# Turning the inputs of three phases with VectorE and DMAs instead of TensorE

## What is computed

```python
h   = norm(x) * gain                      # with modulation: norm(x) * gain * (1 + scale) + shift
hdn = (silu(h @ w_gate) * (h @ w_up)) @ w_down
x   = x + 0.5 * norm(hdn) * gain_post
# second block
mod     = silu(c)     @ ada_w + ada_b     # 9 vectors of 1024
mod_ctx = silu(c_ctx) @ ada_w + ada_b
x   = macaron_ffn(x, mod[0:3], ...)
ctx = macaron_ffn(ctx, mod_ctx[0:3], ...)
h_f, h_b = context_states(ctx, mod_ctx[3:6], ...)
x   = mix_sublayer(x, mod[3:6], h_f, h_b, ...)
x   = macaron_ffn(x, mod[6:9], ...)
```

## Time and profile before

| | us |
|---|---|
| median of three runs | 1662.7 |
| lowest and highest | 1661.25, 1665.88 |
| profiled execution | 1663.65 |
| its span, first to last instruction | 1661.9 |
| granted TensorE clock in it | 1.000 |

### The profile page before, as it was taken

One profiled execution on the slowest core, in us unless ns is written; L12 is line 12 of the kernel. 1 busy time (PEld: TensorE's weight loads), 2 busy tenths in 40 slices (PEclk: granted clock), 3 DMA queues, 4 the chain that ended last, 5 costly groups with the idle time before them and its releaser, 6 DMA issues.

```text
span 1661.9 us, 22791 instructions
## 1 busy us (share of the span) xinstructions
PE 1651.5 (99%) x8748; PEld 1419.4 (85%) x8748; DVE 1217.4 (73%) x1632; ACT 925.1 (56%) x1396; POOL 156.2 (9%) x210
## 2 busy tenths in 40 slices
PE   9999999999999999999999999999999999999998
PEld 7888888888888888888899888888888889988887
DVE  6888776788888767776688776655765668986564
ACT  6655577554545455455566455554555558665553
POOL 1100100000311000120010010100002012310000
PEclk9999999999999999999999999999999999999999
DMA  8977553787859876687646457654667646357561
GB/s 293 337 261 256 170 197 103 240 293 257 285 169 328 272 249 222 246 303 257 201 161 198 164 177 265 199 183 147 219 217 245 195 137 203 111 177 245 181 198 65
DMA packets 99356, 358.47 MB, mean 216 GB/s; under 512 B 11184, under 2 KB 11696, under 8 KB 99248
## 3 DMA queue, kind: packets, MB, share of 16 engines
q1 hardware_dynamic: 92736, 334.73, 60.1%
q0 software_dynamic: 6368, 22.21, 4.1%
q10 hardware_dynamic: 144, 0.07, 0.0%
HBM read 355.85 MB, written 1.12 MB: 215 GB/s over the span
## 4 chain that ended last, share of the span: by engine, by line
PE 94%; DMA 2%; DVE 2%; ACT 1%; issue 0%; SPq 0%; DVEq 0%; POOLq 0%; POOL 0%; ACTq 0%
PE dn L573 28%; PE gu L503 19%; PE tp L544 10%; PE gu L544 10%; PE tp L551 5%; PE gu L551 5%; PE dn L518 5%; DMA raw<-in_weights 2%; PE tp L531 1%; PE gu L531 1%; PE tp L466 1%; PE dn L544 1%; DVE w_lo L1829 1%; PE gu L518 1%; DVE w_lo L1836 1%; PE tp L536 1%
## 5 line engine op out<-in xcount | busy, mean ns | idle before, releaser
L1836 DVE TENSOR_TENSOR w_lo<-raw,w_hi 128x1024 fp32r<-128x1024 f32 x518 | 633.6, 1233 | 302.4 <-ACT w_hi L1195 298.4
L1195 ACT ACTIVATE w_hi<-raw 128x1024 fp32r<-128x1024 f32 x520 | 547.7, 1056 | 436.6 <-PE gu L551 146.1
L503 PE MATMUL gu<-w_hi,hT 128*128 128x512 f32 x1056 | 328.9, 393 | 1.6 <-DVE w_lo L1829 1.1
L573 PE MATMUL dn<-w_hi,actT_hi 128*128 128x512 f32 x608 | 238.6, 392 | 0.0
L573 PE MATMUL dn<-w_lo,actT_hi 128*128 128x512 f32 x608 | 236.8, 390 | 0.0
L573 PE MATMUL dn<-w_hi,actT_lo 128*128 128x512 f32 x608 | 236.8, 390 | 0.0
L503 PEld LDWEIGHTS gu<-w_hi,hT 128*128 128x128 f32 x1056 | 195.5, 188 | 43.1 <-DVE hT L1844 1.7
L503 PE MATMUL gu<-w_lo,hT 128*128 128x512 f32 x528 | 205.8, 390 | 0.0
L544 PE MATMUL tp<-hT,w_hi 128*128 128x512 f32 x736 | 183.3, 391 | 1.1 <-DVE actT_lo L1844 1.0
L544 PE MATMUL gu<-hT,w_hi 128*128 128x512 f32 x736 | 174.8, 390 | 0.0
L544 PEld LDWEIGHTS gu<-hT,w_hi 128*128 128x128 f32 x736 | 137.8, 188 | 28.6
(11 more groups left out here) (366 smaller groups left out, 1986.2 us busy)
## 6 DMA issues: line engine op xcount, KB each, us to landing
raw<-in_weights SPq DMA_DIRECT2D x561, 512.0 KB, 4.3
arena<-in_ada_w SPq DMA_DIRECT2D x72, 512.0 KB, 4.4
post_row<-in_post_rows POOLq DMA_DIRECT2D x10, 512.0 KB, 5.7
pre_row<-in_pre_rows POOLq DMA_DIRECT2D x10, 512.0 KB, 7.0
mod_row<-mod POOLq DMA_DIRECT2D x9, 512.0 KB, 8.6
shift_row<-mod POOLq DMA_DIRECT2D x5, 512.0 KB, 9.3
x<-in_x_in SPq DMA_DIRECT2D x4, 256.0 KB, 5.6
arena<-in_c_rows POOLq DMA_DIRECT2D x2, 512.0 KB, 8.9
```

Source lines behind the costliest of these rows:

```text
L503: m = pe.matmul(bank, h[:, k, t * P:(t + 1) * P], w[:, r, kk * 512:(kk + 1) * 512], start=k == 0 and q == 0, stop=k == KT - 1 and q == 2)
L573: m = pe.matmul(dn[:, t, c], a[:, k, :], w[:, r, c], start=start and q == 0, stop=stop and q == 2)
L1195: act.activation(o, i, ACT.Copy, **kw).then_inc(done, 1)
L1836: dve.tensor_tensor(w_lo[:, r, :], raw[:, n % RAW, :], w_hi[:, r, :].bitcast(F32), ALU.subtract).then_inc(lo_ready, 1)
```

## The change

Three phases are called `APART`: ctx_ffn, ffn_2 and ctx_mix. For them, in the phase before:

- VectorE scales, normalises and transposes the rows in place in 32x32 blocks (`turned_in_blocks`), one or two operations a step in steps 7, 8 and 9, placed behind the reductions (`ahead`).
- SyncE stores the two tiles (512 KB each) to HBM, one after the load at slot LAST - 9 and one after that at LAST - 3, and after that at LAST - 1 waits for both stores and issues four loads of 256 KB that put the blocks in place in xT, in the arena. A load reads runs of 1 KB.
- Partition c * 32 + i of xT holds feature c * 256 + k * 32 + i for tile k, so the host reorders the rows of the gate, up and mixer input weights of these phases to match (`by_blocks`).
- TensorE's `transposed` and the wait between its two blocks go. In the tail it does both tokens' down products and activation transpositions in one loop.
- ScalarE's upper copies and VectorE's subtractions read xT in SBUF instead of PSUM, and ScalarE waits for all four loads. VectorE's split of the second half of the activations comes before the input split of t = 1, no longer behind it.
- ScalarE's squares of the next input move from step 8 to step 4.
- Steps 7 and 8 of ffn_1 do one reduction instead of two, later ones slide, and the first modulation group is turned after step 4 instead of 6.

```diff
+APART = [s for s in EARLY if s - 1 in FFNS]
+APART_STEP = STEPS - 4
-        ADA_IN[_s, _j] = list(range(_done, min(_done + 2, ADA_N)))
+        _n = 1 if _s == FFNS[1] and _j in (APART_STEP, APART_STEP + 1) else 2
+        ADA_IN[_s, _j] = list(range(_done, min(_done + _n, ADA_N)))
-ADA_TURN = {(FFNS[1], 6): 0, (FFNS[2], 8): 1, (FFNS[3], 9): 2}
+ADA_TURN = {(FFNS[1], 4): 0, (FFNS[2], 8): 1, (FFNS[3], 9): 2}
...
+        xT = part(4480, TT, BLOCKS, KT * BLOCK)
...
+        def in_half(s, t, half):
+
+            if s in APART:
+                return xT[:, t, :, :].rearrange("p a (k j) -> p k a j", k=KT)[:, 4 * half:4 * half + 4, :, :]
+            return in_bank(s, t, half).rearrange("p (k a j) -> p k a j", k=4, a=BLOCKS)
...
+            def turned_store(s, t):
+                sp.wait_ge(blocks_turned, TT * APART.index(s) + t + 1)
+                sp.dma_start(turned[bass.ts(t, P), :], xn[:, t, :]).then_inc(turned_stored, 16)
+
+            def turned_load(s):
+                sp.wait_ge(turned_stored, 16 * TT * (APART.index(s) + 1))
+                rows = turned.rearrange("(t a i) (c m) -> c i t a m", t=TT, a=BLOCKS, c=BLOCKS)
+                for c in range(BLOCKS):
+                    sp.dma_start(xT[c * BLOCK:(c + 1) * BLOCK, :, :, :], rows[c]).then_inc(turned_landed, 16)
...
+                    if s + 1 in APART:
+                        if n in (LAST[s] - 9, LAST[s] - 3):
+                            turned_store(s + 1, (n - LAST[s] + 9) // 6)
+                        if n == LAST[s] - 1:
+                            turned_load(s + 1)
...
-                    transposed(s + 1, 0)
-                    for kk in range(2):
-                        down_slot(end + 4 + kk, tokens_of(actT_hi, actT_lo, [0]), kk, used=False)
-                    half_transposed(STEPS - 1, 0)
-                    hT_there(s + 1, 0)
-                    transposed(s + 1, 1)
-                    for kk in range(2):
-                        down_slot(end + 4 + kk, tokens_of(actT_hi, actT_lo, [1]), kk)
-                    half_transposed(STEPS - 1, 1)
+                    for t in range(TT):
+                        for kk in range(2):
+                            down_slot(end + 4 + kk, tokens_of(actT_hi, actT_lo, [t]), kk, used=t == 1)
+                        half_transposed(STEPS - 1, t)
...
             def in_half_upper(s, t, half):
+                if s in APART:
+                    act.wait_ge(turned_landed, 16 * BLOCKS * (APART.index(s) + 1))
...
-                    if j == STEPS - 3 and s + 1 in EARLY:
+                    if j == 4 and s + 1 in APART:
                         for t in range(TT):
                             in_squares(s + 1, t)
...
+            def turned_in_blocks(s, t):
+                dve.wait_ge(xn_ready, TT * (s - 1) + t + 1)
+                dve.transpose(xn[:, t, :], xn[:, t, :]).then_inc(blocks_turned, 1)
...
+                def ahead(j, q):
+                    if s + 1 not in APART:
+                        return
+                    if j == APART_STEP:
+                        if q == 0:
+                            scaled_apart(0)
+                        else:
+                            normalised(s + 1, 0)
+                    if j == APART_STEP + 1:
+                        if q == 0:
+                            turned_in_blocks(s + 1, 0)
+                        else:
+                            scaled_apart(1)
+                    if j == APART_STEP + 2:
+                        if q == 0:
+                            normalised(s + 1, 1)
+                        else:
+                            turned_in_blocks(s + 1, 1)
...
                         ada(j, 0)
+                        ahead(j, 0)
                         after_slots(n, 1)
                         gates_summed(j)
                         after_slots(n + 1, 2)
                         ups_summed(j)
                         ada(j, 1)
+                        ahead(j, 1)
...
                     in_lower(s + 1, 0)
                     half_lower(STEPS - 1, 0)
                     after_slots(end + 3, 1)
+                    half_lower(STEPS - 1, 1)
                     in_lower(s + 1, 1)
                     after_slots(end + 4, 1)
-                    half_lower(STEPS - 1, 1)
```

More of the change, by code:

```diff
@@ L79 @@
 EARLY = [s for s in range(1, len(SUB)) if SOURCE[s] != s - 1]
+APART = [s for s in EARLY if s - 1 in FFNS]
+TURNED_N = {s: 2 * TT * len([q for q in range(s) if q not in APART]) for s in range(len(SUB))}
+BLOCK = 32
+BLOCKS = P // BLOCK
+APART_STEP = STEPS - 4
 NORMS = [("pre", 0, t) for t in range(TT)]
@@ L136, with build @@
 MIX0 = {"ab": 0, "sc": MIX_AB, "ssd": MIX_AB + MIX_SC}
-def build(nc, weights, ada_w, x_in, ctx_in, pre_rows, post_rows, small, mod, out):
+def build(nc, weights, ada_w, x_in, ctx_in, pre_rows, post_rows, small, mod, turned, out):
     with ExitStack() as stack:
@@ L1258, in in_half_upper @@
             def in_half_upper(s, t, half):
-                act.wait_ge(hT_psum, 2 * (TT * s + t) + half + 1 if s else FIRST_HT[t, half])
-                copy(hT_hi[:, 4 * half:4 * half + 4, t * P:(t + 1) * P],
-                     in_bank(s, t, half).rearrange("p (k c) -> p k c", k=4), hT_hi_ready)
+                if s in APART:
+                    act.wait_ge(turned_landed, 16 * BLOCKS * (APART.index(s) + 1))
+                else:
+                    act.wait_ge(hT_psum, TURNED_N[s] + 2 * t + half + 1 if s else FIRST_HT[t, half])
+                copy(in_half_to(hT_hi, t, half), in_half(s, t, half), hT_hi_ready)
             def in_upper(s, t):
@@ L1404, in ffn @@
                     act_upper(STEPS - 2)
-                if s + 1 in EARLY:
+                if s + 1 in APART:
                     after_slots(end, 3)
@@ L2042, in ada, with scaled_apart @@
                         ada_sums(i)
+                def scaled_apart(t):
+                    if s + 1 in MOD:
+                        in_scaled(s + 1, t)
+                def ahead(j, q):
[14 more added lines that the diff above has]
+                            normalised(s + 1, 1)
+                        else:
+                            turned_in_blocks(s + 1, 1)
                 def first_opening():
@@ L2676, in narrow, with by_blocks, swiglu_slots @@
     return slot
-def swiglu_slots(w_gate, w_up, w_down, turned=True):
+def by_blocks(w):
+    return w.reshape(BLOCKS, KT, BLOCK, -1).transpose(1, 0, 2, 3).reshape(D, -1)
+def swiglu_slots(w_gate, w_up, w_down, turned=True, apart=False):
+    if apart:
+        w_gate, w_up = by_blocks(w_gate), by_blocks(w_up)
     slots = []
@@ L2700 @@
            ffn2_w_gate_2, ffn2_w_up_2, ffn2_w_down_2):
-    first = swiglu_slots(ffn1_w_gate_2[0], ffn1_w_up_2[0], ffn1_w_down_2[0])
+    first = (ffn1_w_gate_2[0], ffn1_w_up_2[0], ffn1_w_down_2[0])
     w_in, dt_at = w_in_2[0], 4 * 256 + 512 + SSD_W + 512
@@ L2709 @@
         "ffn_1": swiglu_slots(ffn2_w_gate[0], ffn2_w_up[0], ffn2_w_down[0]),
-        "ctx_ffn": first,
-        "ffn_2": swiglu_slots(ffn1_w_gate[1], ffn1_w_up[1], ffn1_w_down[1]),
+        "ctx_ffn": swiglu_slots(*first, apart=True),
+        "ffn_2": swiglu_slots(ffn1_w_gate[1], ffn1_w_up[1], ffn1_w_down[1], apart=True),
         "sc": [mixed_columns(c_in, [k * D + i * P for i in range(KT) for k in (1, 2, 0)]), c_w_out[0]],
-        "ctx_mix": [narrow(w_in[:, dt_at:]), columns(w_in[:, 1024 + 512:dt_at])],
+        "ctx_mix": [narrow(by_blocks(w_in[:, dt_at:])), columns(by_blocks(w_in[:, 1024 + 512:dt_at]))],
         "ffn_3": swiglu_slots(ffn2_w_gate[1], ffn2_w_up[1], ffn2_w_down[1]),
-        "ffn_4": first,
+        "ffn_4": swiglu_slots(*first),
         "ssd": [wide(w_in[:, :512]), wide(w_in[:, 512:1024]), narrow(w_in[:, dt_at:]), mixed_columns(w_in, [1024 + i * P for unit in XBC_UNITS[1] for i in unit]),
@@ L2778 @@
     mod = nc.dram_tensor("mod", [ADA_N, 2, P], F32, kind="Internal").ap()
+    turned = nc.dram_tensor("turned", [TOK, D], F32, kind="Internal").ap()
     out = nc.dram_tensor("out", [TOK, D], F32, kind="ExternalOutput").ap()
     build(nc, aps["weights"], aps["ada_w"], aps["x_in"], aps["ctx_in"], aps["pre_rows"], aps["post_rows"],
-          {name: aps[name] for name in small_arrays}, mod, out)
+          {name: aps[name] for name in small_arrays}, mod, turned, out)
     nc.compile()
```

6 lines of the change are left out of this document (4 added, 2 removed).

## The result

The changed kernel takes 1667.4 us (median of 7 runs, 1664.7 to 1669.6), the kernel before 1662.95 beside it on the same chip (7 runs): ratio 1.003, 95% interval [1.002, 1.004]. Forecast were 1659.6 us and a range of 1657.0 to 1666.5. The profiled execution took 1667.38 us with a span of 1665.6; before it was 1663.65 and 1661.9, so the two profiles differ by 3.7 us.

A forecast was written before the change was run, and what follows sets the result against it. TensorE, busy 1651.5 of 1661.9 us, was taken as the bound. From the profiled 1663.65 us, +0.35 - 1.75 - 1.75 = -3.15 gives 1660.5, and the median lies 0.95 below that execution: 1659.6 us, range 1657.0 to 1666.5.

The forecast's parts named there:

- What bounds the kernel, the ceiling: TensorE bounds the kernel; removing two transposition blocks in each of three tails saves at most 5.2 us, 1.75 a tail.
- VectorE's turn: Steps 7 to 9: a 32x32 transposition pass on VectorE takes 1.2 us, at most 2.4, and costs TensorE nothing.
- The moves: Squares to step 4, modulation group after step 4, scaling earlier, reductions shifted: no cost; any modulation shortfall paid once.
- the third rival: Tails: copies from the turned tile slower than from PSUM; doubled, they add 1.2 us a tail, 1663 us; chance 0.08.
- Where TensorE arrives early: Tails into next openings: VectorE's list makes ffn_1 +0.35 us; ctx_ffn and ffn_2 keep -1.75 each.
- The wait of "some 2 us": In ctx_ffn's opening, the first token-turning pair waits some 2 us for VectorE's gate product; in ffn_2's it doesn't.
- The round trip: Tails: second store issued at 459 to 461, loads landed at 467 to 475, taken as 470.5 in ffn_1, in time.
- T: Start of a tail's first block of transpositions, 469.12 in ffn_1; the reference for landing times.
- The first rival: Late round trip in the tails: each us beyond T + 1.9 costs one at all three; worst 1671 us; chance 0.27.
- point of decision: Late loads cost time only from a landing at T + 1.9 on; earlier landings are free.
- some 12 us from store to need: Tails: time available between the store and the copies' need of the loads, given as evidence against a late round trip.

The follow-up runs named there:

- e1: The changed kernel with its loads reading x_in rows, not waiting for the stores, five slots earlier; three phases get wrong inputs: 1659.72 us, ratio 0.9985.
- e3: The changed kernel with the round trip cut by token tile, tile 0 loaded six places earlier behind its own store: 1659.84 us, ratio 0.9982.
- e10: e3 with one VectorE reduction kept in each of ffn_1's steps 9 and 10: 1658.06 us, ratio 0.9973.
- e6: The kernel before with only the moved work of the change, TensorE still transposing: 1662.08 us, ratio 0.9994.
- e8: The changed kernel with the two weight loads behind the second store held until the round trip's loads are issued: 1673.02 us, one run.
- e5: The changed kernel with four more loads (768 KB, to an unused place) ahead of the real ones in each tail: 1681.45 us, ratio 1.0115.
- e11: The changed kernel with the second store issued one place earlier, ahead of the weight load just before it: 1667.35 us, ratio 1.0031.
- e2_list: The changed kernel with the two reductions of ffn_1's step 10 done in its steps 7 and 8: 1666.89 us, ratio 1.0026.

## Why the prediction was wrong

**What bounds the kernel, the ceiling.** Right. TensorE without the blocks is 1.8 us earlier per tail, in one case 2.3, where neither the loads nor VectorE's list are late (e1, e3), and e10 has 5.5 us in the stretches and 4.1 in the medians, of a ceiling of 5.2.

**VectorE's turn.** Right: 1.24 us each, against 1.2 taken, and no product waited for it. The Trainium skill (VectorE: DVE Perf Modes, "Rules for kernel authors") prefers TensorE for a 128x128 transposition; the change lost, but not for VectorE's price: with the same six turns e3_split is faster than before.

**The moves.** Right: nothing (e6, 0.9994). ScalarE's copies from the turned tile take 613 to 634 ns each, against 593 to 620 from PSUM in the same tails before, and VectorE's splits 681 to 693, against 678 to 684: the third rival is out.

**Where TensorE arrives early.** Right, and more exactly than I had claimed: +0.35 in ffn_1 was +0.4 and +0.2 in e1 and e3, -1.75 in ctx_ffn was -1.8 twice, -1.75 in ffn_2 was -2.3 and -1.8. The wait of "some 2 us" was 2.0 and 1.8.

**The round trip.** This step failed, by its size. Three terms of it, for ffn_1:
- The store "landed at 462 to 465.5", which is 2.6 to 4.3 us. It took 6.4 us, 5.6 and 5.4 in the others, from 459.03, at the early end of the issue times. The 2.6 us were those of the `out` store, issued when the program has nothing else under way. Even with no load behind it the store took 4.9 to 6.5 (e8).
- The loads I put at 5.2 to 9.7 us and near the lower end. From first issue to last landing they took 7.6, 9.3 and 8.9.
- The reason for the lower end, "the DMA engines stand idle in that stretch", was read wrongly. The tenths of the earlier trace rows from 462 to 470 are idle only from some 465 on. SyncE's weight loads fill the part before, in which the store travels. The part that was idle did stay free for the trip's loads, but that made them no quicker: they fill the engines by themselves, at 220 to 243 GB/s.

Together 14 us from issue to landing instead of the 9.5 to 11.5 that I had, and the landing at T + 4.8 instead of T + 1.4 (470.5 with T at 469.1). In sentences that stood apart, I had an estimate by the Trainium skill (DMA: Bandwidth & Descriptors, cost table), 7.6 us for both legs; the trace shows 14.0 to 14.9, about twice that, and e8 still 12 to 14. The page gives that table for transfers that GpSimd issues, and these are SyncE's. The measurement decides: the estimate is no time for a trip in traffic, and no lower bound either, since the `out` store took 2.6 us where the table makes 3.2.

**The first rival.** Its mechanism, its sign (copies of hT that wait for a DMA) and its point of decision were right, and its price of one us for each nearly so (above, behind e5). Late by 2.9, 3.3 and 1.9 us beyond T + 1.9, less the 1.75 + 1.75 - 0.35 otherwise gained, gives 8.1 - 3.15 = +4.95; the medians differ by 4.4, the spans by 3.7. I gave it 0.27. The true case lay in the upper part of my own bounds, which ran to T + 5.9; "some 12 us from store to need" was told as evidence against it and was just what 12 to 14 us for the trip itself make too little.

**What stays open.** Why a 512 KB store takes 5 to 6 us in a tail and 2.6 at the end of the program. One of e11's stores took 2.7, and it is the one before which SyncE had issued nothing for 2.6 us, while a load was issued 0.4 to 1.2 us ahead of the others. That points to the load just ahead, but it is one case, noticed afterwards. And why the trip's loads move at 220 to 243 GB/s where weight loads reach 399. Each goes to 32 partitions, weight loads to 128; no run here varies the number of loads or of partitions, so that is a guess. What can be said is what it is not: not the size of the pieces, and, in the middle of the loads, not weight loads beside them.

## What to carry to other kernels

Price a DRAM round trip on the path as a whole, from the issue of the store to the last landing, by transfers that run in the same traffic, and compare it with the time from issue to need; the lower ends of bounds taken from other transfers were too short together here, and idle engines were no reason to choose them. If it doesn't fit, cut it by tile so that most of it leaves early; sending the same late request a little sooner doesn't help when another load goes out in the gap. And look at TensorE's granted clock before pricing a long wait: after those of 5 to 7 us in e5 it was at half for a while, and that came on top. And when TensorE is relieved, look for the engine whose list has no gap behind it: a gain arrives only if that list is shortened as well, here by taking one or both of a tail's reductions out of it.

## What the runs showed of the hardware

- VectorE turns all 32x32 blocks of a 128x1024 fp32 tile in 1.24 us, the time of a plain pass over the same elements.

```profile
455.69 1.24 DVE L1918 STREAM_TRANSPOSE xn<-xn 128x1024 f32<-128x1024 f32 x1
```

- A 512 KB store on SyncE's queue took 2.6 us with nothing beside it. The second stores of the tails took 4.9 to 6.8, with or without weight loads behind them, but for the one of 2.7 in e11 and one of 8.2 in e1_early, issued while its four loads were still under way.
- Four loads of 256 KB, each to 32 partitions, took 7.6 to 9.3 us from the first issue to the last landing in the changed kernel, 7.1 to 7.8 in e8_weights_held and 7.3 to 10.2 in e2_list; 8.1 to 8.4 with 8 KB in a row for each partition; 11.2, 10.0 and 13.5 behind three weight loads (e11).
- In the middle of such loads the DMA engines moved 220 to 243 GB/s with 1 KB pieces and 216 with 8 KB, at a full share, and 399 GB/s with weight loads and a store (462 to 465.5).
- After TensorE waits of 5.0 to 6.8 us the granted clock stood at 0.50 for 6.8 us, three times in e5; after waits of up to 2.3 us in the changed kernel's profile it stayed at 1.00.
- ScalarE and VectorE read the turned tile in runs of 32 elements nearly at the pace at which they read PSUM: 0.62 us against 0.60 for 128x512 on ScalarE, 0.68 us either way on VectorE.
